# Gated linear attention in a decoder step: the order of work between the last gate projections, the chunk recurrence and the eight sample rows

## The reference, cut to what matters

```
# prompt: 4 chunks of 64 tokens, per head (4 heads, dk 128, dv 256)
o = att(q, k, decay) @ v + (q * exp(b)) @ S       # within the chunk, and across from the state
S = exp(b_end) * S + (k * exp(b_end - b)).T @ v   # S is 128 x 256 per head
# sample: one step for each of 8 sequences, with its own state from HBM
S_b = exp(g) * S_b + k_b outer v_b ;  o_b = q_b @ S_b
# both
o = rms_norm(o, gnorm) * silu(r) ;  x = x + gate * (o @ w_out)
```

## Time and profile before

| | us |
|---|---|
| median of three executions | 1714.7 |
| the profiled execution | 1710.45 |
| its span | 1708.6 |
| TensorE busy | 1617.0 (95%) |
| VectorE busy | 707.4 (41%) |
| ScalarE busy | 445.1 (26%) |
| GpSimd busy | 146.3 (9%) |

### The profile page before, as it was taken

The page is one execution under the profiler, slowest core; times in us unless marked ns, Lnnn a source line. Parts: engine busy times, 40 slices in busy tenths (PEclk is TensorE's granted clock), DMA queues, the critical chain, the costliest instruction groups (busy, mean ns, idle before and its releaser), DMA issues. The chain is left out here.

```text
span 1708.6 us, 30812 instructions
## 1 busy us (share of the span) xinstructions
PE 1617.0 (95%) x11730; PEld 953.4 (56%) x11730; DVE 707.4 (41%) x1918; ACT 445.1 (26%) x995; POOL 146.3 (9%) x206
## 2 busy tenths in 40 slices
PE   5999899999999999999989988989999999999997
PEld 4677566555545555554457656655555554555554
DVE  2133426563333323333335963175533333333334
ACT  2211103122223222222232134032232222223223
POOL 0000300000000000000020043000000000000000
PEclk9899889999999999999999989899999999999999
DMA  9975537799999999999683443548999999999990
GB/s 360 355 263 170 207 119 285 317 390 394 416 416 416 416 412 416 413 416 415 266 298 108 176 144 112 185 182 337 395 415 416 416 416 414 415 413 416 412 372 26
DMA packets 139032, 552.38 MB, mean 323 GB/s; under 512 B 19407, under 2 KB 36637, under 8 KB 104662
## 3 DMA queue, kind: packets, MB, share of 16 engines
q1 hardware_dynamic: 120562, 513.82, 75.7%
q0 software_dynamic: 15392, 34.66, 5.8%
q10 hardware_dynamic: 3012, 3.00, 0.5%
HBM read 562.74 MB, written 8.60 MB: 334 GB/s over the span
## 5 line engine op out<-in xcount | busy, mean ns | idle before, releaser
L1432 PE MATMUL PS<-ring,arena 128*64 128x256 f32 x4288 | 489.1, 381 | 2.5 <-ACT arena L1762 1.5
L1432 PEld LDWEIGHTS PS<-ring,arena 128*64 128x64 f32 x4288 | 303.3, 137 | 181.8 <-issue 40.0
L1456 PE MATMUL PS<-ring,arena 128*64 128x512 f32 x1072 | 259.6, 605 | 1.4 <-ACT arena L1747 1.4
L1395 PE MATMUL PS<-arena 128*128 128x512 bf16 (+1 forms) x796 | 197.4, 384 | 0.0
L1664 DVE TENSOR_TENSOR arena<-arena,PS 128x128 f32<-128x128 f32 x134 | 38.6, 288 | 369.9 <-ACT arena L1745 364.0
L1648 DVE TENSOR_SCALAR arena<-arena 128x512 bf16<-128x512 f32 x130 | 62.8, 483 | 256.6 <-ACT arena L1756 256.6
L1755 ACT COPY arena<-PS 64x512 f32<-64x512 f32 x134 | 77.6, 579 | 302.2 <-PE PS L1456 302.2
L1456 PEld LDWEIGHTS PS<-ring,arena 128*64 128x64 f32 x1072 | 65.1, 136 | 120.4 <-issue 104.0
L1745 ACT ACTIVATE arena<-PS 128x128 f32<-128x128 f32 x134 | 37.2, 278 | 324.5 <-PE PS L1432 324.5
L1395 PEld LDWEIGHTS PS<-arena 128*128 128x128 bf16 (+1 forms) x796 | 69.6, 99 | 91.8 <-issue 27.7
L1386 PEld LDWEIGHTS PS<-cst,arena 128*128 128x128 f32 x552 | 72.0, 195 | 80.2 <-issue 78.3
(11 more groups left out here) (512 smaller groups left out, 1559.0 us busy)
## 6 DMA issues: line engine op xcount, KB each, us to landing
ring<-in_moe_w_gate SPq DMA_DIRECT2D x134, 1024.0 KB, 7.9
ring<-in_moe_w_up SPq DMA_DIRECT2D x134, 1024.0 KB, 10.3
ring<-in_moe_w_down SPq DMA_DIRECT2D x134, 1024.0 KB, 15.5
ring<-in_w_ada SPq DMA_DIRECT2D x32, 1152.0 KB
ring<-in_w_ada SPq DMA_DIRECT2D x16, 768.0 KB
ring<-in_gla_w_in SPq DMA_DIRECT2D x8, 1152.0 KB
ring<-in_dsa_w_in SPq DMA_DIRECT2D x6, 1024.0 KB
arena<-in_state_gla POOLq DMA_DIRECT2D x8, 512.0 KB, 5.9
```

What stands on the lines that cost most here:

```text
L1395: ins_ = pe.matmul(PS[:, c, :], oh[:, T * P:(T + 1) * P], y[:, 512 * j:512 * j + 512], start=False, stop=True, skip_group_check=True)
L1432: m = pe.matmul(PS[64 * half:64 * half + 64, 5, 0:256].rearrange("p (g n) -> p g n", g=2), rows[:, k, CAP * b:CAP * b + CAP], gu[:, :, k, ...
L1456: m = pe.matmul(PS[64 * j:64 * j + 64, 7, :], hTt[b][:, kk * CAP:(kk + 1) * CAP], ring[:, s, 2, kk * D + 512 * j:kk * D + 512 * j + 512], ...
```

## The change

Nothing is computed differently; instructions are moved, banks and one buffer are changed.

- The sample rows are turned in step 0, into banks 6 and 7, in place of step 3. The turned k goes to banks 4 and 5.
- The steps after them come one gate tile earlier: updates(0) after tile 19, within(0) after 20, across(1) with updates(1) after 21. After tile 22 now come within(1), across(2) and outer(0), after tile 23 outer(1) and across(3).
- The sums of the second token half are in banks 2 and 3. Even outer products use banks 6 and 7.
- `on[0]` and `on[1]` lie in a third of a weight slot that is free then, and the wait for tile 24 of the projection is gone.
- VectorE takes `kmask` before the scores and state 2 before `dve_on(0)`; ScalarE takes the norm of half 0 between gate tiles 21 and 22; GpSimd scales the gate in two halves and loads sample states 5 to 7 between them, state 4 behind.

```diff
-        on = [hT...[:, D * T:D * T + (D if T < 2 else GDV)] for T in range(TT)]
+        on = [ring[:, it_gout[0][0], 2, D * T:D * T + D] for T in range(2)] + [hT...[:, 2 * D:2 * D + GDV]]
...
             elif step == 3:
-                pe.wait_ge(S("gla_dve"), GD["v_tok"] + 2)
-                for h in range(GH):
...
+                pe.wait_ge(S("gla_dve"), GD["att_out"] + 2)
+                pe_updates(0)
             elif step == 4:
-                pe.wait_ge(S("gla_dve"), GD["kmask"] + 1)
-                pe_updates(0)
+                pe_within(0)
             elif step == 5:
-                pe_within(0)
+                pe_across(1)
+                pe_updates(1)
             elif step == 6:
-                pe_across(1)
+                pe.wait_ge(S("state"), 3)
+                pe_within(1)
+                pe_across(2)
+                pe.wait_ge(S("on_ready"), 1)
+                pe_outer(0)
             elif step == 7:
-                pe_updates(1)
+                pe.wait_ge(S("state"), 4)
+                pe_outer(1)
+                pe_across(3)
...
         def pe_gla_rest():
-            pe_within(1)
-            pe_across(2)
-            pe_across(3)
-            pe.wait_ge(S("state"), 4)
+            pe_outer(2)
             pe.wait_ge(S("proj_act"), 8)
...
-            pe_outer(0)
-            pe_outer(1)
             pe_turn_on(0, 0, 1, 1)
             pe_sample_o(0)
-            pe_outer(2)
-            pe_turn_on(0, 1, 1, 1)
             pe_sample_o(1)
             pe_outer(3)
-            pe_turn_on(1, 0, 6, 2)
-            pe_turn_on(1, 1, 7, 2)
+            pe_turn_on(0, 1, 1, 1)
+            pe_turn_on(1, 0, 2, 2)
+            pe_turn_on(1, 1, 3, 2)
             pe_sample_o(2)
...
             dve_state(1)
+            dve_state(2)
             dve_on(0)
-            dve_state(2)
             dve_state(3)
             dve_sample(0)
             dve_sample(1)
+            dve_sample(2)
             dve_on(1)
             dve_mix(0, 0, 1)
-            dve_sample(2)
+            dve_sample(3)
             dve_mix(0, 1, 1)
-            dve_sample(3)
...
             dve.wait_ge(S("o_rms"), T + 1)
-            if T == 0:
-                dve.wait_ge(S("proj"), 24)
...
-            for m_ in range(16, 24):
+            for m_ in range(16, 22):
+                gate(m_)
             for T in range(TT):
+                if T == 1:
+                    gate(22)
+                    gate(23)
+                    act.wait_ge(S("on_ready"), 1)
...
+            scale_gate(0)
+            pool.wait_ge(S("across"), 2)
+            for b in range(5, DEC):
+                load_state(b)
+            scale_gate(1)
             pool.wait_ge(S("state"), 4)
             pool.wait_ge(S("across"), 3)
-            for b in range(4, DEC):
+            load_state(4)
```

More of the change, by code:

```diff
@@ L704, in build @@
         qm = rstd[:, 0:256].rearrange("p (h b c) -> p h b c", h=GH, c=DEC)
-        on = [hT.rearrange("p k t -> p (k t)")[:, D * T:D * T + (D if T < 2 else GDV)] for T in range(TT)]
+        on = [ring[:, it_gout[0][0], 2, D * T:D * T + D] for T in range(2)] + [hT.rearrange("p k t -> p (k t)")[:, 2 * D:2 * D + GDV]]
         oms, ors = modA[:, 0, :], modA[:, 1, :]
@@ L789, in pe_gla_core @@
                     m.then_inc(S("gla_pe"), 1)
+                for h in range(GH):
+                    q = slice(64 * (h % 2), 64 * (h % 2) + DEC)
+                    pe.matmul(PS[q, 6, (h // 2) * P:(h // 2 + 1) * P], pT[:, 4 + h, SEQ:TOK], K["ident"], start=True, stop=True)
+                    for v in range(2):
+                        m = pe.matmul(PS[q, 7, (h // 2) * GDV + v * P:(h // 2) * GDV + (v + 1) * P], pT[:, 8 + 2 * h + v, SEQ:TOK], K["ident"], start=True, stop=True)
+                m.then_inc(S("gla_pe"), 1)
             elif step == 1:
-                pe.wait_ge(S("gla_dve"), GD["kd"] + 1)
+                pe.wait_ge(S("gla_dve"), GD["v_tok"] + 2)
                 for T in range(2):
                     for h in range(GH):
-                        m = pe.transpose(PS[:, 6 + T, h * P:(h + 1) * P], kd[:, h, T * P:(T + 1) * P], K["ident"])
+                        m = pe.transpose(PS[:, 4 + T, h * P:(h + 1) * P], kd[:, h, T * P:(T + 1) * P], K["ident"])
                     m.then_inc(S("gla_pe"), 1)
             elif step == 2:
-                pe.wait_ge(S("gla_dve"), GD["v_tok"] + 1)
                 for T in range(2):
@@ L974, in dve_gla @@
                 dve.tensor_copy(vtok[:, T, :], PS[:, 2 + 2 * T:4 + 2 * T, :].rearrange("p b n -> p (b n)")).then_inc(S("gla_dve"), 1)
+            dve.wait_ge(S("gla_pe"), GP["kv8_T"] + 1)
+            for o in range(2):
+                r = slice(64 * o, 64 * o + DEC)
+                dve.tensor_copy(vv[r], PS[r, 7, :].rearrange("p (j v) -> p j v", j=2))
             for T in range(2):
                 dve.wait_ge(S("gla_pe"), GP["kd_T"] + T + 1)
-                dve.tensor_copy(kdt[:, T, :], bank(6 + T)).then_inc(S("gla_dve"), 1)
+                dve.tensor_copy(kdt[:, T, :], bank(4 + T)).then_inc(S("gla_dve"), 1)
+            for o in range(2):
+                r = slice(64 * o, 64 * o + DEC)
+                ins_ = dve.tensor_tensor(kmask[r], bc(PS[r, 6, 0:256].rearrange("p (j n) -> p j n", j=2), 1, DEC),
+                                         K["fold"][r, 0:DEC].unsqueeze(2).unsqueeze(3).broadcast_to([DEC, DEC, 2, P]), ALU.mult)
+            ins_.then_inc(S("gla_dve"), 1)
             for T in range(2):
```

63 lines of the change are left out of this document (27 added, 36 removed).

## The result

The changed kernel takes 1699.6 us (median of 8 executions, 1695.53 to 1705.51), the kernel before on the same chip 1711.91 (8 executions, 1708.66 to 1716.13). The ratio is 0.9921 with an interval of [0.9902, 0.994]: faster by 0.8%, 13.5 us with an interval of 10.3 to 16.8 (the two medians themselves lie 12.3 apart). Profiled against profiled, the span went from 1708.6 to 1696.4: 12.2 us.

What follows compares the result with a forecast made beforehand. TensorE's path to the output projection was taken as the bound: 41.2 us after the last tile become 26.7, the tile ends 4.2 later, gain 10.3; from median 1714.7 to 1704.4, own range 1701.5 to 1708, whole range 1697 to 1710.

Steps and rivals of the forecast that it cites:

- its own case: Sample tail partly at 2.4 GHz, as before: output projection at 212.4, gain 10.3 us (7 to 13), chance 0.53.
- a sign of being right: Output projection on TensorE beginning at 211 to 214 us, instead of 222.70.
- a sign of being wrong: TensorE clock of 1.00 at 196 to 206 us; output projection would then begin near 208.
- The chunk stretch: TensorE up to the last gate tile: 2.31 us wait goes, 6.55 of work added, tile ends at 185.7, no stall.
- The second norm: Last tile to first mix: across(3) done 188.6, root 191.8 including an added 1.28 us table load, mix 194.4.
- The sample tail: First mix to output projection: gain 7.8 all at 1.2 GHz, 14.7 to 16.0 at 2.4, 10.3 in pieces.
- the piece: One return to 2.4 GHz in the sample tail, after dense transposes: about 1.3 us on each of two samples, 2.5.
- GpSimd and state 4: Sample state 4 issued at 189.1 behind gate scaling, landing 193.5 to 196.7; cover at least 1.3 us.
- One to one to the end: TensorE paces everything behind the output projection's start, so the gain there carries in full to the kernel's end.
- The half-eaten gain: Rival: clock already down when across(3) ends; gain 5.5 us, or 2.5 with state 4 late; 1709 to 1712, chance 0.19.
- The other side: Rival: half clock reaches into the chunk stretch; from updates(0) on, the kernel would take 1731 us; chance 0.05.
- The high clock through the tail: Rival: TensorE stays at 2.4 GHz through the sample tail; gain about 16 us, 1698.7; chance 0.13.

Runs made afterwards that it cites:

- The first part alone: Kernel before, with only the sample rows turned in step 0 and VectorE taking `kmask` ahead of the scores: ratio 0.998, median 1711.07 us.
- the 64-row kernel: Changed kernel with outer products over 64 rows instead of 8, `kmask` zero in the added rows: ratio 0.9902, median 1683.75 us on a faster chip (before 1701.51).
- the second profile of the changed kernel: Changed kernel run once more without an edit: median 1702.5 us, ratio 0.9913; stage from projection tile 16 to output projection 78.53 us, not 72.67.
- the blocks without a gap: Changed kernel plus five gapless blocks of extra matmuls behind the sample tail (full, 8-row, full, 8-column, full): clock 0.50 in the 8-row block; no kernel time given.
- the kernel with the late norm: Changed kernel with outer(0) and outer(1) behind the last tile and ScalarE's norm of half 0 behind all silus: ratio 0.9959, 1707.42 us.
- one variant: Changed kernel with the second half's sums in banks 6 and 7 again, even samples' outer products in 2 and 3: ratio 0.9924, 1699.17 us.
- both kernels that removed it: Early root table, `dve_on(1)` and first mix before sample 2, own state 4 buffer: on changed kernel with four fill matmuls 0.9926; on 64-row outer products without fill 0.9893.

## Why the prediction was right, and where it was off

1704.4 was forecast with 1701.5 to 1708 for its own case and 1697 to 1710 over all; 1699.6 was measured, inside the whole range and 1.9 below that of its own case. The mechanism was right; one term was too small, and the reason given for that term was wrong. The output projection began at 209.71, or 210.4 with the 0.68 put back, earlier than the 211 to 214 that I had named as a sign of being right, and the clock of 1.00 at 196 to 206, a sign of being wrong, was there until 200.

- *The chunk stretch.* Last gate tile done at 185.7 forecast, with the wait of 2.31 gone and 6.55 of work added. Measured 185.23, which is 185.91 on the scale of before once the 0.68 ahead of the stage is put back. The first part alone showed the 2.31 by itself.
- *The second norm.* across(3) forecast done at 188.6, the root's end at 191.8, the first mix's end at 194.4, TensorE waiting 1 to 2. Measured 188.2, 191.5, 194.0 and 1.67. The table load cost 1.28 and no drain beside it: 0.02 between load and root. The Trainium skill's drain of 1.38 (ScalarE: Activation LUTs, What ACT_TABLE_LOAD costs) would have put the root 1.4 later; the trace disagrees again.
- *The sample tail.* From the last tile to the output projection I had worked out 22.3 at 2.4 GHz throughout, 29.2 at 1.2, and 26.7 for the case I took, with one piece worth 2.5. The three ways were sized well: the 64-row kernel took 184.97 to 206.97, 22.0; the second profile of the changed kernel 190.32 to 218.98, 28.7. The first profile took 185.23 to 209.71, 24.5. So the step that was off is the size of the piece at 2.4 GHz: half of the tail and not two samples, 4.2 less than all-slow and not 2.5. With the profiled gain at 12.3 and the one by the ratio at 13.5, this term carries the difference to 10.3, as far as one execution can show. It isn't a constant either: between two executions of one kernel it was worth all of its 4. That the time came out so near is partly luck, since which share of the tail an execution runs at 2.4 GHz was not something that I could work out.
- *The reason given for it fell.* I let the piece hang on the twelve transposes. Both profiles of the changed kernel have them in the same place, and the clock stood at 1.00 behind them in one and at 0.50 in the other. What brings it down in the tail is the outer products over 8 rows: a block of them does it without a gap, and with 64 rows in their place the clock stays at 1.00 in the same tail. The Trainium skill (TensorE: Matmul & The Clock Gate, HAM oscillation) lays the fall on idle gaps in TensorE; the blocks without a gap show a fall that the rule doesn't cover, which is also why closing the gaps left the half clock in the tail. But idle gaps have a part here too, which I had not read: before, the clock was down already at 188, directly behind the wait of 3.37 (the row below), and back at 1.00 in 192 to 194. The first part alone (0.50 in 186 to 188, behind a wait of 3.36) and the kernel with the late norm (0.60 behind 3.46) show the same. In the changed kernel, where that wait is gone, the clock is 1.00 there and within(1) takes 1.89 and not 2.55.

```profile
188.00:190.00 2.00, 2.00 (x6) 1.04 (x6) 0.37 (x1) 0.00 (x0) 0.00 (x0) 0.54 1.03 410
```

- *GpSimd and state 4.* Issue forecast at 189.1, landing 193.5 to 196.7, cover at least 1.3. Measured 188.80, 196.7 and 0.6. The landing times of the earlier trace rows were no bound: state 4 took 7.9, and the slowest load 12.6. The weight load that might go ahead of it did (185.20 against 188.80). The 3 us that I had put on that case come from no row; state 4 landed 0.3 later than the 7.6 of the earlier trace rows would have it. It cost nothing here, and 0.35 in one variant.
- *One to one to the end.* 12.3 in the stage, 12.2 in the span, and the weight queue's waits are 811.6 where they were 809.1.
- *The rivals.* The half-eaten gain (0.19) wanted a low clock at across(3), which no profile of the changed kernel has. The other side (half clock in the chunk stretch) didn't come: the outer products between tiles are single ones, and the clock is 1.00 there. The high clock through the tail (0.13) is what the 64-row form brings about.
- *The base.* The median of 1714.7 was of three executions; of eight it is 1711.91. 2.8 of the 4.8 us between forecast and result are this, and have nothing to do with the change.

How the gain divides, by the ratios, which are from several chips and each uncertain by 0.2% or more: about 0.2% for the rows first, 0.4% for the place of the norm, and nothing that can be measured for the outer products among the tiles and the banks. The rest, about 0.2%, was not taken apart: moving the chunk steps one tile up was not tried alone.

Open: what decides how much of the tail an execution runs at 2.4 GHz. Two profiles of one kernel differ in little else. Forms with row counts between 32 and 64 were not tried, nor a norm without a root on ScalarE.

## What to carry to other kernels

A norm or another small chain that needs only part of the data should stand where that part is complete, even at the price of a table load; look for an engine that sat idle for long before a short instruction (15.04 us before a reciprocal here) and ask what really held it. Where TensorE is busy and slow, look at the form of the matmuls as well as at the gaps, and try padding thin contractions with zeros. Before a new order is tuned further, check which engine sets the pace behind the wait: the wait for the first mix, once removed, came back one hand-over later in both kernels that removed it.

## What the runs showed of the hardware that was not expected

- Matmuls of 128x256 fp32 that contract over 8 or 32 rows brought the granted clock from 1.00 to 0.50 with TensorE busy all the time, and held it there for some 45 us; over 64 rows, of whose weights 63 were zeros, it stayed at 1.00. Eight output columns in place of 128 did no harm.
- At 1.00 the fp32 matmul of 128x256 over 64 rows took 0.436 us (27.89 for 64); the one over 8 rows, mostly at 0.50, took 0.79 (50.56 for 64). At the same clock of 1.00 the four matmuls of an outer product take 1.13 over 8 rows and 1.13 or 1.14 over 64: fewer rows are not faster.
- Two profiled executions of one kernel differ by 5.9 us in this stage through the clock alone; executions of it spread from 1692.67 to 1708.58.
- A table load runs ahead of the wait of the activation that wants it, as the switch back to silu shows in the changed kernel's timeline of ScalarE: the load starts at once behind the root, the silu 1.20 us after the load's end.

```profile
174.21 1.28 ACT L1078 ACT_TABLE_LOAD   x1
176.70 0.39 ACT L1078 ACTIVATE arena<-PS 128x264 f32<-128x264 f32 x1 [1.20 <-PE PS L757]
```

- The same 512 KB loads issued by GpSimd landed in 4.4 to 7.6 us in one order of the program and in 4.3 to 12.6 in another (up to 12.9 in its second profile).
